# Another order for scales, sigmoids, sums and weight remainders in two gated projections of a 16-stage transformer kernel

## The reference, cut to what matters

```python
for i in range(DEPTH):                       # 2 layers
    hn = rmsnorm(h, norm_mix[i])
    ...                                      # short convolution (layer 0) or dilated attention (layer 1)
    h = h + mixed
    h = h + squared_relu_mlp(rmsnorm(h, norm_mlp[i]), mlp_w_up[i], mlp_w_down[i])
    ple_gate = jax.nn.sigmoid(rmsnorm(h, norm_ple[i]) @ ple_w_gate[i])    # 1024 x 1024
    h = h + ple_gate * (p[i] @ ple_w_proj[i])                             # p: 256 x 256, w: 256 x 1024
```

## Time and profile before

| | |
|---|---|
| runs, us | 1891.36, 1895.96, 1906.11 (median 1895.96) |
| the profiled execution, us | 1891.75 |
| its span, us | 1889.9 |
| TensorE busy, us | 1834.3 |
| VectorE busy, us | 1289.2 |
| ScalarE busy, us | 929.5 |
| GpSimd busy, us | 639.5 |
| granted clock, mean | 0.986 |
| HBM traffic over the span | 177 GB/s |

### The profile page before, as it was taken

The page is one execution under the profiler, slowest core; times in us unless marked ns, Lnnn a source line. Parts: engine busy times, 40 slices in busy tenths (PEclk is TensorE's granted clock), DMA queues, the critical chain, the costliest instruction groups (busy, mean ns, idle before and its releaser), DMA issues.

```text
span 1889.9 us, 31756 instructions
## 1 busy us (share of the span) xinstructions
PE 1834.3 (97%) x13378; PEld 1696.4 (90%) x13395; DVE 1289.2 (68%) x1504; ACT 929.5 (49%) x1216; POOL 639.5 (34%) x756
## 2 busy tenths in 40 slices
PE   8999999899999999999999889999999999999999
PEld 7889999899999899988998788999889999788998
DVE  7878676766664777676666856666656666756665
ACT  5354445444344544455444245445554545765443
POOL 6968881486763788110000630000000002520000
PEclk9999999999999999999999999999999999799999
DMA  6556655454444465647555415666345553014552
GB/s 264 178 184 218 217 205 189 154 179 166 157 168 166 156 218 207 223 160 319 190 184 199 174 47 195 222 212 220 137 137 201 197 205 135 23 49 178 198 181 109
DMA packets 53786, 336.35 MB, mean 178 GB/s; under 512 B 7899, under 2 KB 11020, under 8 KB 16908
## 3 DMA queue, kind: packets, MB, share of 16 engines
q1 hardware_dynamic: 46272, 300.00, 44.3%
q10 hardware_dynamic: 3276, 19.64, 2.7%
q0 software_dynamic: 4096, 14.68, 2.3%
HBM read 318.54 MB, written 15.75 MB: 177 GB/s over the span
## 4 chain that ended last, share of the span: by engine, by line
PE 83%; DVE 9%; ACT 5%; issue 2%; POOL 1%; DMA 1%; SPq 0%; ACTq 0%; DVEq 0%; POOLq 0%
PE psum L545 23%; PE psum L481 13%; PE psum L483 13%; PE psum L482 13%; PE psum L547 12%; DVE w_lo L2013 3%; ACT w_hi L1203 2%; DVE both L2020 1%; ACT both L1203 1%; PE psum L1106 1%; PE psum L1010 1%; PE psum L972 1%; PE psum L1104 1%; DVE h L2026 1%; PE psum L1123 1%
## 5 line engine op out<-in xcount | busy, mean ns | idle before, releaser
L2013 DVE TENSOR_TENSOR w_lo<-raw,w_hi 128x2048 fp32r<-128x2048 f32 x277 | 653.5, 2361 | 183.4 <-ACT w_hi L1203 181.5
L545 PE MATMUL psum<-both,w_hi 128*128 128x512 f32 x1984 | 708.7, 399 | 11.2 <-DVE both L2020 6.9
L1203 ACT ACTIVATE w_hi<-raw 128x2048 fp32r<-128x2048 f32 (+1 forms) x281 | 534.6, 1904 | 178.0 <-PE psum L483 171.4
L547 PE MATMUL psum<-both,w_lo 128*128 128x256 f32 x1984 | 560.4, 282 | 0.0
L481 PE MATMUL psum<-both,w_hi 128*128 128x256 f32 x1600 | 460.2, 288 | 18.5 <-DVE both L2020 9.8
L545 PEld LDWEIGHTS psum<-both,w_hi 128*128 128x128 f32 x1984 | 375.3, 189 | 100.5 <-DVE both L2020 7.9
L483 PE MATMUL psum<-both,w_lo 128*128 128x256 f32 x1600 | 451.2, 282 | 0.0
L482 PE MATMUL psum<-both,w_hi 128*128 128x256 f32 x1600 | 451.1, 282 | 0.0
L547 PEld LDWEIGHTS psum<-both,w_lo 128*128 128x128 f32 x1984 | 376.1, 190 | 0.1
L481 PEld LDWEIGHTS psum<-both,w_hi 128*128 128x128 f32 x1600 | 303.3, 190 | 18.6 <-DVE both L2020 11.4
L482 PEld LDWEIGHTS psum<-both,w_hi 128*128 128x128 f32 x1600 | 304.4, 190 | 0.6 <-issue 0.2
(11 more groups left out here) (406 smaller groups left out, 2463.8 us busy)
## 6 DMA issues: line engine op xcount, KB each, us to landing
raw<-in_weights SPq DMA_DIRECT2D x279, 1024.0 KB, 4.8
table<-tables ACTq DMA_DIRECT2D x8, 1792.0 KB, 9.1
tables<-st POOLq DMA_DIRECT2D x16, 512.0 KB, 4.1
tables<-st POOLq DMA_DIRECT2D x8, 256.0 KB, 6.4
tables<-turns POOLq DMA_DIRECT2D x8, 256.0 KB, 4.5
w<-in_cmp_w ACTq DMA_DIRECT2D x4, 512.0 KB, 5.3
tbl<-in_cmp_w ACTq DMA_DIRECT2D x4, 512.0 KB, 5.4
tbl<-bias_v SPq DMA_DIRECT2D x128, 16.0 KB, 4.8
```

What stands on the lines that cost most here:

```text
L545: nc.tensor.matmul(bank, wh[:, cols], both[x][:, c, 0:2 * SEQ], start=c == 0, stop=False, skip_group_check=True)
L547: return nc.tensor.matmul(bank[:, 0:SEQ], wl[:, cols], x_hi[x][:, c], start=False, stop=c == KC - 1, skip_group_check=True)
L1203: copy = lambda out, in_, **kw: nc.scalar.activation(out, in_, ACT.Copy, **kw)
L2013: tt(w_lo[:, g % RING], raw[:, g % RING], w_hi[:, g % RING].bitcast(F32), ALU.subtract).then_inc(sem["lo_ready"], 1)
```

## The change

What moves, stage by stage:

- **End of both MLPs.** VectorE's `last_sums` takes a new argument `late`: the split of the first gate unit stands before `x_low` of the last pair, where it stood behind it.
- **ScalarE in ple0 and ple1.** Before: split of gate unit 3, copy of `rs`, then for each pair sigmoid, split, residual (`x_high` and squares). After: splits of gate units 3 and 4, copy of `rs`, sigmoids 0 and 1, a split, residuals 0 and 1, sigmoid 2, a split, residual 2, sigmoid 3, residual 3, the last split.
- **VectorE in ple0 and ple1.** Before: for each pair scale, `x_low` of the pair before, product, sum, split, an angle group (layer 0). After: the order in the diff below. `angles(0)` and `angles(1)` stand ahead of the norm, `angles(2)` under sigmoid 0, `angles(3)` behind the last sum. Gate unit 4 is split between the norm and the first scale. The low parts of pairs 0 and 1 stand behind scale 2, that of pair 2 behind scale 3.

No computing instruction is added or taken away on any engine; SP's loads keep their order.

```diff
--- before.py
+++ after.py
@@ -1378,15 +1378,24 @@
 
             def ple(l, n, r):
                 g = BASE[f"ple{l}"]
-                split(g)
-                norm(n)
-                for m in range(PAIRS):
+                def sigmoid(m):
                     act.wait_ge(sem["gate_scaled"], PAIRS * l + m + 1)
                     nc.scalar.activation(tb[:], ta[:], ACT.Sigmoid).then_inc(sem["gate_ready"], 1)
-                    if m < PAIRS - 1:
-                        split(g + 1 + m)
-                    residual(r, m)
-                split(g + PAIRS)
+
+                split(g)
+                split(g + 1)
+                norm(n)
+                sigmoid(0)
+                sigmoid(1)
+                split(g + 2)
+                residual(r, 0)
+                residual(r, 1)
+                sigmoid(2)
+                split(g + 3)
+                residual(r, 2)
+                sigmoid(3)
+                residual(r, 3)
+                split(g + 4)
 
 
             act_fn = nc.scalar.activation
@@ -2065,7 +2074,7 @@
                         split(BASE[stage] + m)
                 split(BASE[stage] + 2)
 
-            def last_sums(g, r, scale, x, banks=DB):
+            def last_sums(g, r, scale, x, banks=DB, late=None):
 
                 for m in range(PAIRS + 1):
                     if m < PAIRS:
@@ -2074,6 +2083,8 @@
                         else:
                             done(g)
                         add(m, two(banks[m]), scale)
+                    if m == PAIRS and late is not None:
+                        split(late)
                     if m and x:
                         x_low(r, m - 1)
 
@@ -2143,8 +2154,7 @@
                         table_inner(4 * l + TABLE_AT[l].index(i - 1))
                     low_part(i)
                     split(g + down_at(i - 2))
-                last_sums(g + 2 * MLP_PAIRS - 1, r, 1.0, True)
-                split(g + 2 * MLP_PAIRS - 2)
+                last_sums(g + 2 * MLP_PAIRS - 1, r, 1.0, True, late=g + 2 * MLP_PAIRS - 2)
                 split(g + 2 * MLP_PAIRS - 1)
 
             def ffn(f, n, r, x=True, late=None, side=None):
@@ -2244,21 +2254,53 @@
 
             def ple(l, n, r):
                 g = BASE[f"ple{l}"]
+                at = PAIRS * l
+                into, by = [DB[3], U[0], U[1], [DB[3], MB][l]], [XB, DB[0], DB[1], DB[2]]
+
+                def scaled(m):
+                    done(g + 1 + m)
+                    tt(ta[:], two(into[m]), rs_b, ALU.mult).then_inc(sem["gate_scaled"], 1)
+
+                def product(m):
+                    dve.wait_ge(sem["gate_ready"], at + m + 1)
+                    if m:
+                        dve.wait_ge(sem["h_ready"], hbase(r) + m)
+                    tt(tc[:], tb[:], two(by[m]), ALU.mult).then_inc(sem["gated"], 1)
+
+                def sums(m):
+                    dve.wait_ge(sem["gated"], at + m + 1)
+                    add(m, tc[:])
+
                 split(g)
+                if l == 0:
+                    angles(0)
+                    angles(1)
                 norm(n)
+                split(g + 1)
                 dve.wait_ge(sem["rs_ready"], n + 1)
-                for m in range(PAIRS):
-                    done(g + 1 + m)
-                    tt(ta[:], two([DB[3], U[0], U[1], [DB[3], MB][l]][m]), rs_b, ALU.mult).then_inc(sem["gate_scaled"], 1)
-                    if m:
-                        x_low(r, m - 1)
-                    gated(PAIRS * l + m + 1, two([XB, DB[0], DB[1], DB[2]][m]), m)
-                    if m < PAIRS - 1:
-                        split(g + 1 + m)
-                    if l == 0:
-                        angles(m)
-                x_low(r, PAIRS - 1)
-                split(g + PAIRS)
+                scaled(0)
+                if l == 0:
+                    angles(2)
+                product(0)
+                scaled(1)
+                sums(0)
+                product(1)
+                sums(1)
+                split(g + 2)
+                scaled(2)
+                x_low(r, 0)
+                x_low(r, 1)
+                product(2)
+                sums(2)
+                split(g + 3)
+                scaled(3)
+                x_low(r, 2)
+                product(3)
+                sums(3)
+                if l == 0:
+                    angles(3)
+                x_low(r, 3)
+                split(g + 4)
 
 
             dve.wait_ge(sem["vec_landed"], 16)
```

## The result

The changed kernel took 1882.4 us (median of 6 runs, 1880.08 to 1885.87) against 1895.37 us (6 runs, 1891.36 to 1906.11): ratio 0.9927, 95% interval 0.9904 to 0.995. It is faster by 0.7%, less than the 1% named as the bound, and 4.1 us under the predicted 1886.5. The profiled execution took 1885.87 us, span 1884.1, granted clock 0.985; it is the slowest of the six.

A forecast was written before the change was run, and what follows sets the result against it. TensorE, busy 97% of the span, was taken as the bound. Gains of 6.3 us in ple0 and 2.5 in ple1 less 1.7 for a clock dip gave 7.1 us; 1886.5 us was named, range 1878 to 1897.

The forecast's parts named there:

- the 1% named as the bound: Whole kernel: 1% (19 us) taken as what a measurement can tell from no change; chance of staying within it 0.88.
- The late remainder: Before the first gate unit: splitting its w_lo earlier removes 1.67 us of TensorE idle in ple0, 0.9 us in ple1.
- The holes around the norm: VectorE and ScalarE idle around the norm takes angles and the fourth gate's weights; norm 1.1 us late in ple0, but hidden.
- Idle inside the qkv unit: First qkv unit of ple0: TensorE waits of 2.0 and 1.8 us remain where 4.93 and 0.33 us were.
- GpSimd's lock: VectorE steps with two SBUF inputs and GpSimd's sums exclude each other; 1.3 us charged at x_low of pairs 0 and 1.
- The new clock dip: After the remaining idle times in ple0's first qkv unit, TensorE's clock falls again, costing 1.7 us.
- Rival (a): No clock dip in ple0, so the change gives 8.8 us, in the middle 1885 us; chance 0.25.
- ple1: Layer 1's gated stage: all three TensorE waits go or shrink, 0.9 + 0.17 + 1.50 = 2.5 us.
- the 0.2 charged to the next norm: End of ple0: the next norm adds 0.2 us because VectorE's w_lo stands before it.
- (b): VectorE stays the bound in ple0, only 2.5 to 3 us gained, in the middle 1891 us; chance 0.13.
- (d): The edit does nothing visible, waits fall elsewhere in the next stage, 1892 to 1896 us; chance 0.10.
- Rival (c): ScalarE's copy of rs waits for the fourth gate's load in both stages; slower, 1902 us at 16 us landings; chance 0.05.

The follow-up runs named there:

- experiment 2: Changed kernel with the late weight remainder put back behind the last x_low; ple0 44.08 us, ple1 44.00 us.
- experiment 5: Changed kernel with angle groups 0, 1 and 2 put back behind the pairs' sums; ple0 43.76 us, ple1 43.29 us.
- experiment 6: Changed kernel with the fourth gate unit's split put back behind the first pair's sum (VectorE) and sigmoid 0 (ScalarE); ple0 43.19 us, ple1 43.91 us.
- experiment 11: Changed kernel with the late remainder ahead of the third pair's x_low and the next stage's second-unit split behind the last x_low; ratio 0.9929 against the kernel before.
- experiment 1: Kernel before with only the late weight remainder moved ahead of the last x_low; ple0 48.29 us, ple1 45.47 us.
- experiment 4: Changed kernel with angles and the fourth gate unit's split put back, keeping late remainder and interleaved pairs; ple0 47.88 us, ple1 43.92 us.
- experiment 8: Changed kernel with four scratch multiplications ahead of layer 0's last x_low to widen the idle time; ple0 49.22 us, ple1 43.28 us.

## Why the prediction was right

- **The late remainder: right.** 1.67 and 0.9 us predicted; 1.79 and 0.76 us by experiment 2. The remainder started at 308.40, and all of ple0's 1.67 us went.
- **The holes around the norm: right.** The norm's first step came at 319.25 and not at 320.1, as VectorE took the lock before GpSimd and both sums ran together under one pair of x_low (310.60, 2.96 us in all). Nothing was lost on the copy of rs. Experiments 5 and 6 price the two hoists.
- **Idle inside the qkv unit: too high.** Predicted 2.0 and 1.8 us, measured 0.28 and 1.57, together 1.95 us less. The mis-sized term is VectorE's chain: the x_low of pair 2 was forecast to end at 341.5 and ended at 339.66. Of these 1.84 us, 0.4 are the start: the norm and scale 0 were 0.8 us early (scale 0 ended at 323.67, not 324.5), and the wait for sigmoid 0 took half of it back. Another 0.4 are GpSimd's lock: it was charged 1.3 us at pairs 0 and 1 and, behind scale 3, 0.6 us at pair 2, and cost 1.04 and 0.44 us, since each sum ran in part beside a scale, which reads one operand from PSUM and is not held up. The last 1.0 us are the steps themselves. The prediction put them end to end at their full length, while in the trace most start 0.08 us before the one ahead ends (scale 2 starts at 331.00 and takes 0.68; x_low starts at 331.60).
- **The new clock dip: wrong.** 1.7 us were taken for it; the granted clock is 1.00 throughout. Rival (a) was right here. Idle times of 1.76 and 1.57 us 3.3 us apart passed without loss in experiment 5, and the one of 1.56 to 1.59 us passed without loss in all eight profiles that have it; 4.43, 4.58, 4.93 and 4.94 us in the same place did not. The price was taken from the idle time of 1.27 us at 122.72. Eleven profiles have it at 1.27 to 1.29 us: in ten the lower clock followed, in experiment 11 (1.28 us) the clock stayed at 1.00. So not even there does the length of the wait decide, and it was no measure for another place.
- **ple1: right,** 2.94 us for 2.5, with 1.28 us left where 1.2 was expected. The listed idle time fell by 2.45 us only. Some 0.3 of the other 0.5 us is that a wait costs more than its listed idle time: in the kernel before matmuls start 0.12 us apart, but 848.80 and 850.59 us stand around a listed 1.50, 0.17 us more than both, and the changed kernel has two such waits fewer. The rest stays open.
- **Sum:** 6.3 + 2.5 - 1.7 = 7.1 us was forecast, 11.45 us came. Of the 4.35 us, 1.7 are the dip, 2.2 are ple0's waits (the 1.95 and the 0.2 charged to the next norm), 0.4 is ple1. The medians differ by 13.0 us; the fastest runs of the two kernels in all rounds, 1891.36 and 1880.01, by 11.35, which agrees with the stages.
- **What the total says.** The range, 1878 to 1897 us, also holds the median of the kernel before, so a time inside it proves little; the rows above carry the verdict. Rival (a), 8.8 us and 1885 in the middle, came nearer to 1882.4 than the forecast of 1886.5, and was itself 2.6 us short.
- **Slips in the prediction's figures.** The middle of 1884.6 and 1888.9 is 1886.75. ple1's three terms add up to 2.57, and TensorE wants its last pair at 848.0, not at 847.8. The 830.8 in the paragraph on ple0 cannot be meant, as that stretch lies at some 330 us. None changes the forecast by more than 0.3 us.
- **Rivals (b) and (d): did not occur.** The last x_low of ple0 started at 342.04 where it had started at 349.79, and the time between the two stages stayed at 454.26 us.
- **Rival (c), a load late for the copy of rs: did not occur.** ScalarE's wait before the copy is 2.23 us, ended by TensorE.

What stays open: whether a change of 10 us in the place of everything behind 850 us moves the odds of the long low-clock stretch. Of the changed kernel's 18 timed runs four lie above 1890; of the kernel before's 45, eleven lie above 1903. The numbers do not tell these apart.

## What to carry to other kernels

Look for idle time on the helping engines ahead of the point where a stage's chain starts (here the norm's scale), and fill it with work that the loop behind that point would do; the order within the loop was worth 3% of the gain on top of that, and 2.0 us where the hoists were missing. Price two moves together as well as apart, since the time that each leaves in reserve is the same time, and the clock comes on top. Name for each wait what holds the engine that ends it: a step that another engine holds up is not a fixed chain. Where single runs scatter by 10 us, compare the length of the changed stage in each profile; it repeats to 0.05 us.

## What the runs showed of the hardware

- A step that reads two operands from SBUF on VectorE and a GpSimd sum exclude each other: 3.38 us for a remainder of 2.28, 2.70 us for four x_low of 1.66, 1.51 us for an angle step of 0.41, and on the other side 1.82 us for a GpSimd sum of 1.29. The angle step L2236 of the kernel before reads one tile and was held up too (1.38 us for 0.29). A scale with one operand in PSUM took its 0.69 us beside a GpSimd sum.
- The price of a 4.4 to 4.9 us idle time in the same place was 1.2 to 4.1 us of extra matmul time (experiments 1, 4, 8 and the kernel before): 3.4 to 10.2 us at the lower level. In experiment 1 the pair behind the hole took 2.93 us (345.56 to 348.82 less 0.33) where it takes 1.69 in the changed kernel.
- An idle time of 1.27 to 1.29 us at one place of the kernel was followed by the lower clock in ten of eleven profiles; the eleventh stayed at 1.00.
- The same 40 us of one kernel's last attention ran at a granted clock of 0.87 in one execution and 0.61 in another. Together with more low clock in shorter stretches elsewhere it went with a span 14.0 us longer (1878.1 and 1892.1 us).
